# Three edits to a fused gated-DeltaNet and sparse-attention trunk: the region's start, the last inverse level on 64x64 blocks, and the order of the norms

## The reference, cut to what matters

```python
q, k = l2norm(q), l2norm(k)                       # x * rsqrt(sum(x*x) + eps), per head and token
gam = cumsum(g);  decay = exp(gam_i - gam_j) for j <= i
a_mat = where(j < i, beta_i * (k @ k.T) * decay, 0)
sol = triangular_solve(eye + a_mat, [v * beta, k * beta * exp(gam)])   # per chunk
u, w = split(sol)
for each chunk:  v_new = u - w @ S;  o = q_dec @ S + qk @ v_new;  S = S * g_last + k_dec.T @ v_new
o = rms_norm(o) * silu(z)
```

## Time and profile before

| | us |
|---|---|
| median of 3 timed runs | 2547.76 (2547.72 to 2549.86) |
| the profiled execution, its time | 2551.24 |
| its span, first to last instruction | 2549.5 |
| TensorE busy | 2417.9 (95%) |
| VectorE, ScalarE, GpSimd busy | 1229.9, 1062.4, 1194.6 |
| mean granted TensorE clock | 0.981 of full |

### The profile page before, as it was taken

One profiled execution on the slowest core, in us unless ns is written; L12 is line 12 of the kernel. 1 busy time (PEld: TensorE's weight loads), 2 busy tenths in 40 slices (PEclk: granted clock), 3 DMA queues, 4 the chain that ended last, 5 costly groups with the idle time before them and its releaser, 6 DMA issues.

```text
span 2549.5 us, 31817 instructions
## 1 busy us (share of the span) xinstructions
PE 2417.9 (95%) x12324; PEld 2011.7 (79%) x12324; DVE 1229.9 (48%) x2232; ACT 1062.4 (42%) x2029; POOL 1194.6 (47%) x856
## 2 busy tenths in 40 slices
PE   6989989899999999999988989889999999999998
PEld 5678878778878888888766878778888788888886
DVE  4775675654452344440146666765454423444402
ACT  5545355355542333332265454453554423333312
POOL 3363553533345555554443654634344455555542
PEclk9999999999999999999989999999999999999998
DMA  3211111022223333333321111110222233333332
GB/s 133 65 37 46 38 42 43 21 66 75 75 72 95 94 95 95 98 97 95 93 64 58 34 46 42 38 38 25 75 76 74 78 95 95 91 99 95 97 94 83
DMA packets 98502, 183.35 MB, mean 72 GB/s; under 512 B 10928, under 2 KB 11056, under 8 KB 98224
## 3 DMA queue, kind: packets, MB, share of 16 engines
q1 hardware_dynamic: 98352, 181.32, 24.8%
HBM read 179.18 MB, written 2.10 MB: 71 GB/s over the span
## 4 chain that ended last, share of the span: by engine, by line
PE 84%; DVE 11%; ACT 2%; issue 1%; POOL 1%; DMA 1%; SPq 0%; DVEq 0%; ACTq 0%
PE bank L1240 81%; PE bank L1306 2%; DVE conv_acc L815 2%; DVE tt L812 1%; PE bank L1508 1%; PE bank L1300 1%; DVE decay L1005 1%; ACT w_hi L494 1%; DVE left L815 1%; DVE ob_lo L812 1%; DVE z_act L815 1%; POOL mt_even L436 0%; DVE qk_t L815 0%; DVE v_f L815 0%; DVE k_dec L812 0%
## 5 line engine op out<-in xcount | busy, mean ns | idle before, releaser
L411 POOL TENSOR_TENSOR w_lo<-w_raw,w_hi 128x512 fp32r<-128x512 f32 x668 | 942.5, 1432 | 1259.3 <-ACT w_hi L494 1259.3
L1240 PE MATMUL bank<-xn_hi,w_hi 128*128 128x512 f32 x1936 | 782.6, 404 | 17.4 <-ACT z_raw L505 6.8
L1240 PE MATMUL bank<-xn_hi,w_lo 128*128 128x512 f32 x1936 | 783.1, 405 | 0.0
L1240 PE MATMUL bank<-xn_lo,w_hi 128*128 128x512 f32 x1936 | 778.9, 402 | 0.2 <-POOL xn_lo L471 0.2
L494 ACT ACTIVATE w_hi<-w_raw 128x512 fp32r<-128x512 f32 x668 | 384.2, 623 | 726.6 <-PE bank L1240 721.6
L1240 PEld LDWEIGHTS bank<-xn_hi,w_hi 128*128 128x128 f32 x1936 | 368.4, 190 | 93.2 <-issue 9.8
L1240 PEld LDWEIGHTS bank<-xn_hi,w_lo 128*128 128x128 f32 x1936 | 369.6, 191 | 73.2 <-issue 5.3
L1240 PEld LDWEIGHTS bank<-xn_lo,w_hi 128*128 128x128 f32 x1936 | 368.7, 190 | 71.2 <-issue 1.5
L815 DVE SCALAR_TENSOR_TENSOR conv_acc<-x_raw,hconv,conv_acc 128x512 f32<-128x512 f32 x144 | 155.0, 1076 | 26.5 <-ACT conv_acc L505 24.0
L812 DVE TENSOR_TENSOR residual<-residual,bank 128x512 f32<-128x512 f32 x32 | 21.9, 685 | 268.1 <-PE bank L1240 267.9
L1240 PE MATMUL bank<-mid_hi,w_hi 128*128 128x512 f32 x352 | 139.2, 396 | 0.0
(11 more groups left out here) (245 smaller groups left out, 3600.7 us busy)
## 6 DMA issues: line engine op xcount, KB each, us to landing
w_raw<-w_tiles SPq DMA_DIRECT2D x668, 256.0 KB, 2.6
residual<-x_t SPq DMA_DIRECT2D x4, 512.0 KB, 5.3
out_t<-normalised SPq DMA_DIRECT2D x8, 256.0 KB, 2.2
rope<-rope SPq DMA_DIRECT2D x1, 1024.0 KB, 10.2
mats<-mats SPq DMA_DIRECT2D x1, 768.0 KB, 7.9
vecs_all<-vecs SPq DMA_DIRECT2D x1, 133.0 KB, 7.7
```

The source lines that it names most:

```text
L411: nc.gpsimd.tensor_tensor(w_lo[j][:], w_raw[j][:], w_hi[j][:].bitcast(F32), ALU.subtract).then_inc(s_lo, 1)
L1240: return nc.tensor.matmul(out, lhsT, rhs, start=start, stop=stop)
```

## The change

1. `X` is rounded up to the next multiple of 128: it moves by 32 bytes, and so does all that lies in the region. What started at 96 now starts at 0, what started at 32 now at 64.
2. At level 6 only the quadrant that can differ is computed: `T5_` transposes the upper left 64x64 of `tt`, `P6_` and `U6_` multiply 64x64 blocks, and the copies and the subtraction take 64 partitions of 4x64 elements.
3. The norm is split: keys' eps, root, inverse, `fac`, `k_b` and `k_dec` come first in VectorE's stream, the queries' later with a root of their own; `z_act` moves behind level 1.

```diff
-        X = place[0]
+        X = -(-place[0] // 128) * 128
...
-                nc.scalar.activation(rinv[:], rinv[:], ACT.Sqrt).then_inc(gdn_a.step("sqrt"), 1)
-                stages("kt", "gb", "ss")
+                nc.scalar.activation(rinv[:, :, 1, :], rinv[:, :, 1, :], ACT.Sqrt).then_inc(gdn_a.step("sqrtk"), 1)
+                stages("kt", "gb")
+                act.wait_ge(gdn_v.sem, gdn_v.after(t, "varq1"))
+                nc.scalar.activation(rinv[:, :, 0, :], rinv[:, :, 0, :], ACT.Sqrt).then_inc(gdn_a.step("sqrtq"), 1)
+                stages("ss")
...
+                evac(f"T{LV[-2]}_", [x[:TOP, :, :TOP] for x in t_m], [chunks(x)[:TOP, :, :TOP] for x in by])
+                evac(f"P{LV[-1]}_", [x[TOP:, :, :TOP] for x in p1], [chunks(x)[:TOP, :, :TOP] for x in bx])
...
+                        rows = TOP if L == LV[-1] else P
+                        tt_(odd_blocks(tt[s], L)[:rows], odd_blocks(tt[s], L)[:rows], odd_blocks(chunks(bz[s]), L)[:rows], ALU.subtract).then_inc(gdn_v.step(f"U{L}_{s}"), 1)
                     stages(f"U{L}_")
+                    if L == 1:
+                        for s in range(2):
+                            dve.wait_ge(gdn_a.sem, gdn_a.after(t, f"ztanh{s}"))
+                            stt(z_act[s][:], z_act[s][:], 1.0, z_raw[s][:], ALU.add, ALU.mult).then_inc(gdn_v.step(f"zact{s}"), 1)
...
+                        if L == LV[-1]:
+                            for c in range(NC):
+                                last = mm(chunks(bx[s])[:TOP, c, :TOP], mt[L % 2][s][:TOP, c, TOP:], t_m[s][:TOP, c, :TOP])
...
+                            if L == LV[-1]:
+                                last = mm(chunks(bz[s])[:TOP, c, TOP:], p1[s][TOP:, c, :TOP], tt[s][TOP:, c, TOP:])
...
+                            if L == LV[-2]:
+                                for c in range(NC):
+                                    last = nc.tensor.transpose(chunks(by[s])[:TOP, c, :TOP], tt[s][:TOP, c, :TOP], ident[:TOP, :TOP])
```

More of the change, by code:

```diff
@@ L322, in hybrid_trunk @@
         gdn_p = steps("gdn_pe", [m for st in STAGES for m in two(st)])
-        gdn_a = steps("gdn_act", two("sqq", "sqk") + ["sqrt"] + two("exp", "kbT", "eg", "ztanh", "T0_")
+        gdn_a = steps("gdn_act", two("sqq", "sqk") + ["sqrtk", "sqrtq"] + two("exp", "kbT", "eg", "ztanh", "T0_")
                       + [m for L in LV for m in two(f"P{L}_", f"T{L}_")][:-2] + two("w", "osq", "o") + ["osqrt"])
-        gdn_v = steps("gdn_dve", ["hcol", "htot"] + two("varq") + ["vark"] + two("ga") + ["rinv", "fac", "fq", "fq2", "kb0", "kd0", "kb1", "kd1"]
-                      + two("vb", "at", "i0_", "qk", "zact") + [m for L in LV for m in two(f"U{L}_")]
+        gdn_v = steps("gdn_dve", ["hcol", "htot", "vark", "rinvk", "fac", "kb0", "kd0", "kb1", "kd1"] + two("varq", "ga", "vb")
+                      + ["rinvq", "fq", "fq2"] + two("at", "i0_", "qk") + [m for L in LV for m in two(f"U{L}_") + (two("zact") if L == 1 else [])]
                       + [m for c in range(NC) for m in two(f"V{c}_", f"S{c}_")][:-2]
@@ L624, in evac @@
                         act.wait_ge(gdn_p.sem, gdn_p.after(t, f"{name}{s}"))
-                        copy(dst[s][:], chunks(src[s]), scale=scale).then_inc(gdn_a.step(f"{name}{s}"), 1)
+                        rows = src[s] if len(src[s].shape) == 3 else chunks(src[s])
+                        copy(dst[s][:], rows, scale=scale).then_inc(gdn_a.step(f"{name}{s}"), 1)
                     stages(name)
@@ L637, in gdn @@
                 evac("T0_", t_m, by)
-                for L in LV:
+                for L in LV[:-2]:
                     evac(f"P{L}_", p1, bx)
                     stages(f"U{L}_")
-                    if L < LV[-1]:
-                        evac(f"T{L}_", t_m, by)
+                    evac(f"T{L}_", t_m, by)
+                evac(f"P{LV[-2]}_", p1, bx)
+                stages(f"U{LV[-2]}_")
+                evac(f"T{LV[-2]}_", [x[:TOP, :, :TOP] for x in t_m], [chunks(x)[:TOP, :, :TOP] for x in by])
+                evac(f"P{LV[-1]}_", [x[TOP:, :, :TOP] for x in p1], [chunks(x)[:TOP, :, :TOP] for x in bx])
+                stages(f"U{LV[-1]}_")
                 evac("w", w_t, by, scale=-1.0)
@@ L1037, in gdn @@
                     last.then_inc(gdn_v.step(f"qk{s}"), 1)
-                for s in range(2):
-                    dve.wait_ge(gdn_a.sem, gdn_a.after(t, f"ztanh{s}"))
-                    stt(z_act[s][:], z_act[s][:], 1.0, z_raw[s][:], ALU.add, ALU.mult).then_inc(gdn_v.step(f"zact{s}"), 1)
                 stages("qk", "T0_")
@@ L1426, in gdn @@
                             pe.wait_ge(gdn_v.sem, gdn_v.after(t, f"qk{s}"))
-                        per_chunk(bx[s], mt[L % 2][s], t_m[s]).then_inc(gdn_p.step(f"P{L}_{s}"), 1)
+                        if L == LV[-1]:
+                            for c in range(NC):
+                                last = mm(chunks(bx[s])[:TOP, c, :TOP], mt[L % 2][s][:TOP, c, TOP:], t_m[s][:TOP, c, :TOP])
+                        else:
+                            last = per_chunk(bx[s], mt[L % 2][s], t_m[s])
+                        last.then_inc(gdn_p.step(f"P{L}_{s}"), 1)
                     d.issue(dense_after[f"P{L}_"])
@@ L1433, in gdn @@
                             one = slice(c, c + 1)
-                            last = mm(odd_blocks(chunks(bz[s])[:, one], L), p1[s][:, c, :], odd_blocks(tt[s][:, one], L))
+                            if L == LV[-1]:
+                                last = mm(chunks(bz[s])[:TOP, c, TOP:], p1[s][TOP:, c, :TOP], tt[s][TOP:, c, TOP:])
+                            else:
+                                last = mm(odd_blocks(chunks(bz[s])[:, one], L), p1[s][:, c, :], odd_blocks(tt[s][:, one], L))
                         last.then_inc(gdn_p.step(f"U{L}_{s}"), 1)
@@ L1439, in gdn @@
                             pe.wait_ge(gdn_v.sem, gdn_v.after(t, f"U{L}_{s}"))
-                            columns(by[s], tt[s]).then_inc(gdn_p.step(f"T{L}_{s}"), 1)
+                            if L == LV[-2]:
+                                for c in range(NC):
+                                    last = nc.tensor.transpose(chunks(by[s])[:TOP, c, :TOP], tt[s][:TOP, c, :TOP], ident[:TOP, :TOP])
+                            else:
+                                last = columns(by[s], tt[s])
+                            last.then_inc(gdn_p.step(f"T{L}_{s}"), 1)
                         d.issue(dense_after[f"T{L}_"])
```

32 lines of the change are left out of this document (18 added, 14 removed).

## The result

The kernel after takes 2525.15 us (median of 4 runs, 2523.60 to 2526.48), beside 2548.81 us for the kernel before in the same comparison. The ratio is 0.9905 with a 95% interval of [0.9888, 0.9923]: 0.95% faster. The forecast was 2503 us with a range from 2484 to 2521. The direction is right, the size is half of what was forecast, and the range misses by 4 us. The profiled execution has a span of 2522.8 us, 26.7 us less than before.

What follows compares the result with a forecast made beforehand. TensorE, busy nearly throughout, was taken to bound the kernel through its waits, low clock and overlong instructions. The terms 15 + 10 + 18 + 2 = 45 us gave 2503 us, 1.8% faster, with a range from 2484 to 2521.

Steps and rivals of the forecast that it cites:

- What bounds the kernel: Whole kernel: TensorE is busy nearly throughout; time comes off only its waits, its lower clock, or its own overlong instructions.
- Where the second loss begins: TensorE's waits: the clock falls to 1.2 GHz behind waits longer than somewhere between 2.3 and 2.8 us.
- Part 1: Region's start: 2208 dense products reading moving operands from the region each get 0.0068 us shorter, 15 us; bounds 0 and 8.
- TensorE fetches in units of 64 bytes: Dense products: a 32-byte offset makes 2048 bytes touch 33 units in place of 32, costing 0.0067 us each.
- those at 64 don't: Region's start, lower bound: only the 1184 products whose operands land at remainder 0 gain, 8 us.
- the rival with nothing from the start: Dense products: mid differs from xn in more than address, so the start gives nothing (2518 us) or half (2510); chance 0.14.
- Part 2: Last level on 64x64: 2.1 us less per pair, 0.9 back for array switches; net 1.2, 10 us over 8 pairs.
- Behind T2 TensorE sets the pace again: 8-tile pairs after T2: the gain stays to the end, 3.0 us for each of six pairs, 18 us.
- Part 3, up to T1: 8-tile pair, keys first: kk starts 4.5 us earlier; T1 waits 0.6 us with no drop in the clock.
- Part 3, T2: the step that failed.: 8-tile pair, level 2: T2 waits 3.0 to 4.4 us but comes 4.1 to 5.5 earlier; 3.0 gained per pair.
- VectorE's debt eats part 3: Rival: one TensorE stall with its low clock is only exchanged for another; part 3 gives 5 us, 2518 us; chance 0.13.
- The 4-tile pair: kbT and kk: ScalarE's copy limits the gain; kk 1 us earlier per pair, 2 us in all; bounds -1 and 4 each.

Runs made afterwards that it cites:

- e12_mg_256: Kernel after with z_act behind level 2, top-k rounds from the second on one level later, and mg and the merge's operands 192 bytes further on: 2497.84 us.
- e5_zact_l2: Kernel after with z_act one level later, behind the subtraction of level 2: 2501.05 us.
- e1_region: Kernel before with the region's start alone rounded up: 2539.32 us against 2550.0, 10.7 us faster.
- e6_x64: Kernel after with the region 64 bytes further on: 2530.74 us.
- e9_x128: Kernel after with the region 128 bytes further on: 2532.37 us.
- e12 to e14: e12_mg_256 and two from the kernel after: weight buffers moved 128 bytes, activations keeping their remainders by 256 (2554.48 us); whole memory moved 128 bytes (2524.50 us).
- e2_corner: Kernel before with the last level on 64x64 alone: 2543.29 us against 2550.0, 6.7 us faster.
- e11_no_corner: Kernel after with z_act behind level 2, top-k rounds from the second on one level later, last level on whole 128x128 chunks: 2509.87 us; with 64x64, 2503.37.
- e16_late_whole: e12_mg_256 with all top-k rounds behind the subtraction of level 3 and the last level on whole 128x128 chunks: 2484.08 us; with 64x64, 2484.73.
- e3_keys: Kernel before with the keys first and z_act behind level 1, nothing else: 2544.69 us against 2550.0, 5.3 us faster.
- e7_zact_old: Kernel after with z_act back in its old place, ahead of level 1: 2514.20 us.

## Why the prediction was wrong, step by step

- **What bounds the kernel**: right. All that was gained came from TensorE's waits, its clock and its own instructions.
- **Where the second loss begins** ("between 2.3 and 2.8 us of wait"): fell. The clock dropped behind a wait of 1.88 us in e12_mg_256, and stayed up behind one of 1.91 in e5_zact_l2. In the kernel after it dropped behind the 1.7 us for mt_odd in two pairs and not in the other four. And the trace of before had the answer: there are 12 waits of 2.8 to 2.9 us in its 8-tile pairs, and behind three of them the clock is not low, so "behind each wait" holds for the pair shown and not for all. The length of one wait doesn't decide it. View: kbT in the next pair of the kernel before, and the stretch behind it.

```profile
1608.23 0.66 PE L1306 MATMUL bank<-mats,k_b 128*128 128x128 f32 x4 [2.82 <-DVE k_dec L812]
```

```profile
1608.20:1611.60 3.40, 2.83 (x20) 2.47 (x21) 3.37 (x6) 2.08 (x5) 1.29 (x2) 1.00 0.00 0
```

- **Part 1**: the cause, the address, is right; the term was mis-sized, 10.0 in place of 15 us. The step that failed is "TensorE fetches in units of 64 bytes", with which a start at 64 would cost nothing. mg gained 4.4 ns, not 6.8, and the merge 1.1 ns in the mean. The bound of 8 us for "those at 64 don't" was near it. e1_region (10.7) measures it, so the rival with nothing from the start fell too; e6_x64, e9_x128 and e12 to e14 put another rule in the unit's place.
- **Part 2**: the term is right in its place, 1.2 us for each 8-tile pair between T5 and w. The three stages are 1.48 us shorter up to the dense product behind each, and about 0.26 goes back at their starts; how much of the forecast's 2.1 and 0.9 this is, is not measured apart. What reaches the end is less in two of three comparisons: 6.7 us alone (e2_corner), 6.5 to 9 (e11_no_corner), about nothing against e16_late_whole, where 0.5 us of each pair's gain goes to VectorE's copies of v_new and the rest to two pairs in which the clock falls otherwise. I said "Behind T2 TensorE sets the pace again", which holds only while VectorE has slack there.
- **Part 3, up to T1**: right. kk was to come 4.5 us earlier and came 4.8; the subtraction of level 1 was to stand at 30.5 rel and stood at 30.2; T1's wait was to be 0.6 us and is none.
- **Part 3, T2: the step that failed.** "T2 comes 4.1 to 5.5 us earlier, and 1.7 us go back to the clock. I take 3.0 us for each 8-tile pair." T2 came 2.8 us earlier. The step assumed that the subtraction of level 2 keeps VectorE's lead of 4.0 us, or gains up to 1.4 more. The lead at level 1 was as forecast, but between the two subtractions z_act took 3.29 us, not 2.62 or less, and the two taps behind it 3.42, not 2.57, while GpSimd was busy throughout (5.00 of 5.00 us in the stretch above). T2's wait was 5.22 us against the 3.0 to 4.4 forecast. The clock took 2.3 us behind it, not 1.7. So part 3 gave 0.5 us in this pair in place of 3.0, and 2.8 to -0.8 us in the six, 4.6 together in place of 18. e3_keys gives 5.3 us for what was to be 20. Why z_act took longer is open: GpSimd was busy throughout beside it before as well (2.60 of 2.60 us). That one stall was exchanged for another I had seen, and gave 0.13 to the rival "VectorE's debt eats part 3", which came true at the 5 us that it named. What I did not ask is what the exchange is worth when z_act isn't moved there: e7_zact_old is 11 us faster.
- **The 4-tile pair**: kk came 1.4 us earlier, with the wait for ScalarE that was named; from kt to the last stage each is 2.0 us shorter, 1.35 by the corner. 0.7 us in place of 1. In e3_keys, with the same wait at kk, they are 0.9 us longer than before each, so that the 0.7 may be where the clock falls.
- **The sum**: 10 + 10 + 6 = 26 us against the 26.7 that the span lost, where 45 were forecast.

## What to carry to other kernels

When work is put off on an engine whose queue is full, write down for each level what stands between one due result and the next, and compare it with what the waiting engine has to do meanwhile; the place with the most slack is found by that table, and not by "later". Here 12 us stood against 7 at T2, with 3.7 us of idle VectorE time ahead of the next subtraction, and moving 3 us of it one level further gave as much as the whole change had. Look at every pair of a trace, not at one: the clock falls behind a wait in some and not in others, and what it takes may be swallowed by the next wait. And align the activations that stream against weights with the weights' buffer, by the difference of their starts.
